# Dilated attention: the modulation's two products of a unit on column tiles, and the minima and sums in a ring of their own

## The reference

```python
DILATED_PATTERNS = ((128, 1), (512, 4), (2048, 16))
...
scores = jnp.einsum('bhrnqd,bhrnkd->bhrnqk', qb, kc, preferred_element_type=jnp.float32)
scores = jnp.where(valid, scores, NEG_INF)
m = jnp.max(scores, axis=-1, keepdims=True)
p = jnp.exp(scores - m)
denom = jnp.sum(p, axis=-1, keepdims=True)
out = jnp.einsum('bhrnqk,bhrnkd->bhrnqd', p, vc.astype(jnp.float32)) / denom
lse = (m + jnp.log(denom))[..., 0]
...
wts = jax.nn.softmax(jnp.stack(lses, axis=0), axis=0)      # over the three patterns
...
# the two layers that follow, l = 0 and 1, for c_act and cc_act
shift, scale, gate = jnp.split((c_act @ w_mod + b_mod)[:, None, :], 3, axis=-1)
```

## Time and profile before

| | |
|---|---|
| median of 3 runs | 5559.16 us (5552.03 to 5563.41) |
| time of the profiled execution | 5556.06 us |
| its span | 5554.0 us |
| TensorE busy | 4897.8 us, 88% of the span |
| mean granted TensorE clock | 0.948 |
| the stage of the change | 951 to 1428 us of the span |

### The profile page before, as it was taken

How to read it: one execution, slowest core, us unless ns; L and a number is a source line. 1 busy time by engine, 2 the same in 40 slices (tenths; PEclk the granted TensorE clock), 3 DMA queues, 4 the chain that set the end, 5 groups by cost and what they waited for, 6 DMA issues and landing times. The chain is left out here.

```text
span 5554.0 us, 67686 instructions
## 1 busy us (share of the span) xinstructions
PE 4897.8 (88%) x26653; PEld 3429.6 (62%) x26653; DVE 2387.1 (43%) x4791; ACT 1598.3 (29%) x3015; POOL 1217.2 (22%) x1271
## 2 busy tenths in 40 slices
PE   5888999999786998699999988969987899989889
PEld 2336887877675765474554576858655734544767
DVE  3221022544564465654552146334556635520554
ACT  2231101544335311222342133034112223421331
POOL 1000011000341011143884000010221438850000
PEclk8998999999897999899999999979999999999999
DMA  5001101232442000010000201230000100002122
GB/s 180 2 15 39 53 30 53 96 105 93 154 146 91 16 1 9 13 54 8 10 12 18 74 31 46 95 117 16 9 9 1 50 20 10 10 16 67 38 69 91
DMA packets 156013, 273.43 MB, mean 49 GB/s; under 512 B 12556, under 2 KB 91700, under 8 KB 155060
## 3 DMA queue, kind: packets, MB, share of 16 engines
q1 hardware_dynamic: 142164, 250.23, 13.2%
q10 hardware_dynamic: 13536, 18.88, 1.0%
HBM read 204.12 MB, written 64.95 MB: 48 GB/s over the span
## 5 line engine op out<-in xcount | busy, mean ns | idle before, releaser
L2312 POOL TENSOR_TENSOR y_t<-y_t,weight_ring 128x512 f32<-128x512 f32 x352 | 446.6, 1289 | 67.9 <-ACT weight_ring L2282 63.3
L1398 DVE TENSOR_TENSOR features_low<-h_t,features_high 128x1024 fp32r<-128x1024 f32 x260 | 304.0, 1171 | 355.1 <-ACT features_high L1363 354.4
L2330 DVE TENSOR_REDUCE y_t<-ps_max 128x2 f32<-128x1024 f32 x256 | 313.3, 1224 | 325.4 <-PE ps_max L2139 325.4
L659 PE MATMUL ps_proj<-weight_ring,h_t 128*128 128x256 f32 x2048 | 448.5, 381 | 2.7 <-PE ps_proj L659 2.2
L659 PEld LDWEIGHTS ps_proj<-weight_ring,h_t 128*128 128x128 f32 x2048 | 388.8, 191 | 57.7 <-issue 5.4
L1335 PE MATMUL ps_proj<-features_high,weights_high 128*128 128x512 f32 (+1 forms) x880 | 346.2, 393 | 59.8 <-DVE features_low L1398 30.5
L1363 ACT ACTIVATE features_high<-h_t 128x1024 fp32r<-128x1024 f32 x260 | 259.7, 1001 | 421.4 <-PE ps_proj L1335 359.5
L1335 PE MATMUL ps_proj<-features_high,weights_low 128*128 128x512 f32 (+1 forms) x880 | 340.6, 387 | 0.0
L1335 PE MATMUL ps_proj<-features_low,weights_high 128*128 128x512 f32 (+1 forms) x880 | 340.1, 387 | 0.0
L1526 PE MATMUL ps_f<-h_t,weight_ring 128*128 128x512 f32 (+1 forms) x640 | 288.7, 586 | 14.4 <-DVE state L1691 14.4
L1549 PE MATMUL ps_s<-qf,kb 64*128 64x128 f32 x3264 | 235.7, 285 | 60.9 <-DVE scores_t L1719 55.5
(11 more groups left out here) (340 smaller groups left out, 9089.6 us busy)
## 6 DMA issues: line engine op xcount, KB each, us to landing
weight_ring<-in_w_in_dram SPq DMA_DIRECT2D x40, 1024.0 KB, 5.9
weight_ring<-in_w_mod_dram SPq DMA_DIRECT2D x48, 512.0 KB, 4.0
x_rows<-h_rows SPq DMA_DIRECT2D x32, 512.0 KB, 6.1
t_rows<-t_rows SPq DMA_DIRECT2D x64, 256.0 KB, 2.3
x_res<-h_rows SPq DMA_DIRECT2D x32, 512.0 KB, 3.2
res<-result SPq DMA_DIRECT2D x48, 264.0 KB, 2.1
res_rows<-res SPq DMA_DIRECT2D x48, 264.0 KB, 3.8
h_t<-v_rows SPq DMA_DIRECT2D x3, 4096.0 KB, 13.9
```

The costliest lines, as they stand in the source:

```text
L659: mm = pe.matmul(ps[u % 4][:, 0:GC], hT[:, k, t * P:(t + 1) * P], w[:, k, :], start=(k == 0), stop=(k == KT - 1))
L1398: dve.tensor_tensor(self.fl[:, s % NB, :, 0:n], self.hT[:, k0:k0 + KS, c0:c0 + n], self.fh[:, s % NB, :, 0:n].bitcast(F32), ALU.subtract). ...
L2312: pool.tensor_tensor(acc[g % 2][:, kv, :], before, pT[s % 3][:, kv, :], ALU.add).then_inc(pa.h, 1)
L2330: ins = dve.tensor_reduce(part[:, g % 2, t, c, :].rearrange("p (v i) -> p v i", v=2)[:, :, i], pM[:, :, 0:n], AXX, ALU.max)
```

## The change

- **Column tiles.** Each of the two products of `modulate` now has a stationary operand of 64 columns (each vector repeated over 32) and writes its own half of the partitions, 0 to 63 and 64 to 127, instead of both summing into all 128. `mrow` has 128 partitions, `keep` adds all 128, and the two halves are summed later: `mr` is loaded in two transfers and `stage_output1` turns and adds it with two products instead of one transpose.
- **The ring.** Minima and sums go into `stat`, four tiles deep. `keep` of a tile's second unit copies its 16 columns into `res`, after waiting for the exponentials of that unit. The wait for the store moves from `minima` to `keep`, ahead of the copy into `res`. SP no longer waits for the exponentials.
- **Score order.** The four score products alternate between lower and upper partitions; before, two lower ones came ahead of two upper ones.
- `store_mod` has four transfers of one row each instead of two.

```diff
@@ stage_dilated
-        cvec = free[:, NM * 4 * GC:NM * 4 * GC + KT * P].rearrange("p (k v c) -> p k v c", v=2, c=P // 2)
-        mrow = env.sb(ctx, "mod2_rows", [HD + 1, 2, GC])
+        cvec = free[:, NM * 4 * GC:NM * 4 * GC + KT * HD].rearrange("p (k v c) -> p k v c", v=2, c=32)
+        mrow = env.sb(ctx, "mod2_rows", [P, 2, GC])
+        stat = env.sb(ctx, "row_stats", [P, 4, 2 * H1])
...
-                for v in range(2):
-                    sp.dma_start(mod_d[l:l + 1, 2 * c:2 * c + 2, v, :],
-                                 mrow[HD * v:HD * v + 1, y % 2, :].rearrange("p (m c) -> p m c", c=P)).then_inc(ms[y % 2].h, 16)
+                for i in range(4):
+                    sp.dma_start(mod_d[i:i + 1, 2 * y:2 * y + 2, :],
+                                 mrow[32 * i:32 * i + 1, y % 2, :].rearrange("p (m c) -> p m c", c=P)).then_inc(ms[y % 2].h, 16)
...
                 sp.wait_ge(pvc.h, pvc.at(u + 1))
-                sp.wait_ge(ex.h, ex.at(4 * (u + 1)))
...
-                for odd in range(2):
-                    for j in range(2):
+                for j in range(2):
+                    for odd in range(2):
...
-                    mm = pe.matmul(pv[u % 2][:, GC:2 * GC], cvec[:, 4 * (x % 2) + k, :, :].rearrange("p v c -> p (v c)"),
-                                   mw[:, x % NM, k, :], start=(i == 0), stop=(i == 1))
+                    mm = pe.matmul(pv[u % 2][HD * i:HD * (i + 1), GC:2 * GC], cvec[:, 4 * (x % 2) + k, :, :].rearrange("p v c -> p (v c)"),
+                                   mw[:, x % NM, k, :], start=True, stop=True)
...
@@ minima(u)
-                if hh == 0 and u >= 4:
-
-                    i = (u // 2) % 2
-                    dve.wait_ge(rs[i].h, rs[i].at(16 * (u // 4)))
...
-                                                 res[:, (u // 2) % 2, H1 * HD + h:H1 * HD + h + 1]).then_inc(sm_.h, 1)
+                                                 stat[:, (u // 2) % 4, h:h + 1]).then_inc(sm_.h, 1)
@@ keep(u)
-                row, got = mrow[:, y % 2, :], pv[u % 2][0:HD + 1, GC:2 * GC]
+                row, got = mrow[:, y % 2, :], pv[u % 2][:, GC:2 * GC]
...
+                if hh == 0 and u >= 4:
+                    i = (u // 2) % 2
+                    dve.wait_ge(rs[i].h, rs[i].at(16 * (u // 4)))
+                if hh == 1:
+                    dve.wait_ge(ex.h, ex.at(4 * (u + 1)))
+                    dve.tensor_copy(res[:, (u // 2) % 2, H1 * HD:RW], stat[:, (u // 2) % 4, :])
                 dve.tensor_copy(res[:, (u // 2) % 2, hh * 4 * HD:(hh + 1) * 4 * HD], pv[u % 2][:, 0:4 * HD]).then_inc(pvc.h, 1)
@@ stage_output1
-            sp.dma_start(mr[:, :], mod_d.rearrange("l m v p -> (l m v) p")).then_inc(md.h, 16)
+            for i in range(2):
+                sp.dma_start(mr[:, i, :], mod_d[2 * i:2 * i + 2, :, :].rearrange("v m p -> (v m) p")).then_inc(md.h, 16)
...
-                    pe.transpose(pM[:, 0:NR], mr[:, :], env.ident[0:NR, 0:NR]).then_inc(mu.h, 1)
+                    for i in range(2):
+                        mm = pe.matmul(pM[:, 0:NR], mr[:, i, :], env.ident[0:NR, 0:NR], start=(i == 0), stop=(i == 1))
+                    mm.then_inc(mu.h, 1)
```

More of the change, by code:

```diff
@@ L799, in store_mod @@
             def store_mod(y):
-                l, c = divmod(y, MH // 4)
                 sp.wait_ge(mk.h, mk.at(4 * y + 4))
-                for v in range(2):
-                    sp.dma_start(mod_d[l:l + 1, 2 * c:2 * c + 2, v, :],
-                                 mrow[HD * v:HD * v + 1, y % 2, :].rearrange("p (m c) -> p m c", c=P)).then_inc(ms[y % 2].h, 16)
+                for i in range(4):
+                    sp.dma_start(mod_d[i:i + 1, 2 * y:2 * y + 2, :],
+                                 mrow[32 * i:32 * i + 1, y % 2, :].rearrange("p (m c) -> p m c", c=P)).then_inc(ms[y % 2].h, 16)
             load_v(0)
@@ L825, in _ @@
                 sp.wait_ge(rs[i].h, rs[i].at(16 * (U // 4)))
-                sp.wait_ge(ms[i].h, ms[i].at(32 * MH // 4))
+                sp.wait_ge(ms[i].h, ms[i].at(64 * MH // 4))
         @block.tensor
@@ L935, in keep @@
                     if y >= 2:
-                        dve.wait_ge(ms[y % 2].h, ms[y % 2].at(32 * (y // 2)))
+                        dve.wait_ge(ms[y % 2].h, ms[y % 2].at(64 * (y // 2)))
                     dve.tensor_copy(row, got).then_inc(mk.h, 1)
+                if hh == 0 and u >= 4:
[4 more added lines that the diff above has]
+                    dve.tensor_copy(res[:, (u // 2) % 2, H1 * HD:RW], stat[:, (u // 2) % 4, :])
                 dve.tensor_copy(res[:, (u // 2) % 2, hh * 4 * HD:(hh + 1) * 4 * HD], pv[u % 2][:, 0:4 * HD]).then_inc(pvc.h, 1)
             dve.tensor_copy(cvec[:, :, :, :], env.csilu[:, 8:24].rearrange("p (v k) -> p k v", v=2)[:, :, :, None]
-                            .to_broadcast([P, KT, 2, P // 2])).then_inc(cw.h, 1)
+                            .to_broadcast([P, KT, 2, 32])).then_inc(cw.h, 1)
             minima(0)
@@ L960, in _ @@
                             act.activation(pr[:, u % 2, 2 * b + j, 0:w * P], sc[:, u % 2, 2 * b + j, 0:w * P], ACT.Exp,
-                                           bias=res[:, (u // 2) % 2, H1 * HD + h:H1 * HD + h + 1], scale=-1.0,
-                                           accum_out=res[:, (u // 2) % 2, H1 * HD + H1 + h:H1 * HD + H1 + h + 1])\
+                                           bias=stat[:, (u // 2) % 4, h:h + 1], scale=-1.0,
+                                           accum_out=stat[:, (u // 2) % 4, H1 + h:H1 + h + 1])\
                                .then_inc(ex.h, 1)
@@ L971, in _ @@
                                    ACT.Copy).then_inc(tc0.h, 1)
-    for s_, c_ in (*((ml[i], 16 * len(range(i, MH, NM))) for i in range(NM)), (mu, MH), (mk, U), (cw, 1), (ms[0], 8 * MH), (ms[1], 8 * MH),
+    for s_, c_ in (*((ml[i], 16 * len(range(i, MH, NM))) for i in range(NM)), (mu, MH), (mk, U), (cw, 1), (ms[0], 16 * MH), (ms[1], 16 * MH),
                    (smm, U), (sm_, 4 * U), (ex, 4 * U), (tm, 2 * U), (tc0, U), (tc1, U), (pvm, U), (pvc, U),
@@ L1013, in stage_output1 @@
         rst = env.sb(ctx, "ya_rstd", [P, 2, NT])
-        mr = env.sb(ctx, "mod2_rows", [NR, P])
+        mr = env.sb(ctx, "mod2_rows", [NR, 2, P])
         mc = env.sb(ctx, "mod_cols", [P, 2, 24, 2])
@@ L1116, in _ @@
                 if v == 2:
-                    pe.wait_ge(md.h, md.at(16))
-                    pe.transpose(pM[:, 0:NR], mr[:, :], env.ident[0:NR, 0:NR]).then_inc(mu.h, 1)
+                    pe.wait_ge(md.h, md.at(32))
+                    for i in range(2):
+                        mm = pe.matmul(pM[:, 0:NR], mr[:, i, :], env.ident[0:NR, 0:NR], start=(i == 0), stop=(i == 1))
+                    mm.then_inc(mu.h, 1)
                 if v == 4:
@@ L1212, in modulation @@
                 bt, bo = env.place["b_mod_2"]
-                link(dve.tensor_tensor(mc[:, :, :, :], pM[:, 0:96].rearrange("p (l m v) -> p l m v", l=2, v=2),
+                link(dve.tensor_tensor(mc[:, :, :, :], pM[:, 0:96].rearrange("p (v l m) -> p l m v", l=2, v=2),
                                        env.vcols[:, bt, bo:bo + 48].rearrange("p (l m) -> p l m", l=2)[:, :, :, None]
@@ L1267, in stage_output1 @@
                    (yb, NT), (yah, NT), (yal, NT), (tm, NT), (tch, NT), (tcl, NT), (sqy, NT), (iny, NT), (pwy, NT), (sqm, NT),
-                   (inm, NT), (pwm, NT), (mma, NT), (mmb, NT), (pa, 2 * NT), (pb, 2 * NT), (st, NT), (mu, 1), (md, 16), (gcs, 2),
+                   (inm, NT), (pwm, NT), (mma, NT), (mmb, NT), (pa, 2 * NT), (pb, 2 * NT), (st, NT), (mu, 1), (md, 32), (gcs, 2),
                    (gtn, 1), (gdn, 64), *((hs[i], 16 * len(range(i, NT, NX))) for i in range(NX)),
@@ L2871, in program @@
         gb_d = nc.dram_tensor("gb_rows", [S, H1 * HD], F32, kind="Internal").ap()
-        mod_d = nc.dram_tensor("mod_rows", [2, 3 * KT, 2, P], F32, kind="Internal").ap()
+        mod_d = nc.dram_tensor("mod_rows", [4, 2 * 3 * KT, P], F32, kind="Internal").ap()
         res_d = [nc.dram_tensor(f"res{p}", [S, RW], F32, kind="Internal").ap() for p in range(3)]
```

## The result

The changed kernel takes 5501.01 us, median of 4 runs (5496.05 to 5515.65), against 5556.34 (5552.03 to 5563.41): a ratio of 0.9904, 95% interval 0.9881 to 0.9926. The forecast was 5506. The profiled execution took 5496.05 us (span 5494.1), 60 us less than that of before, of which some 54 lie in the stage and 6 in the rest of the program. The rest, from the last `values` product to the end, took 4123 to 4140 us in the ten profiles of this study, the kernel before at 4130 and the changed one at 4123, so those 6 us are no effect of the change that these profiles could show. The stage is taken here from the start of its first score product to the start of its last `values` product: 472.0 us before, 418.1 after.

A forecast was written before the change was run, and what follows sets the result against it. TensorE was taken as the bound, stalled once per tile by the store wait; 27.8 + 26 - 1.5 = 52.3 us off the profiled 5556.06 gives 5503.8, or 5506 against the median of the runs; range 5492 to 5526.

The forecast's parts named there:

- What bounds the stage: TensorE, 88% busy; each tile's store wait on VectorE delays minima, exponentials, ScalarE's copy and the weight loads of `values`.
- the chain through ScalarE: Minima, exponentials and ScalarE's copy ahead of `values`: ready some 1.4 us before TensorE once the store wait is gone.
- The rival of a late load of `w_mod` behind V: Tile 20's modulation waits for its load behind V, or `keep` meets a late store; 5515 to 5524; 12 in 100.
- The moved wait: Moving the store wait from `minima` to `keep` should cover all of it, gaining 27.8 us over the stage's tiles.
- The column tiles: Modulation products run side by side, 0.27 us less per unit on TensorE, 26 us over 96 units.
- The three terms: Per unit of modulation: 0.48 us less between starts, against 0.10 for the shape change and 0.11 for the first weight load.
- The sum of the two: Gains of the moved store wait, 27.8 us, and of the modulation on column tiles, 26 us, added together.
- Score order: Alternating lower and upper score products was costed at nothing, since two already run at a time.
- The strided scores: Rival: the new order also speeds up score products of dilation 4 and 16, 41 us, giving 5465; 4 in 100.
- The small ones: Additional transfers on SP, and one more transfer and product in `stage_output1`, lose 1.5 us; the 16-column copy is covered.
- The ring: The 27.8 us gain forecast for moving the store wait from `minima` to `keep`.

The follow-up runs named there:

- e3: The changed kernel with the two lower-half score products ahead of the two upper-half ones, as before; 5506.68 us in one run.
- e5: The changed kernel with the keys of every score product read without a stride (other data, timing only); 5479.6 us in one run.
- e6: The changed kernel with keys and queries of the score products both read without a stride (other data, timing only); 5458.16 us in one run.
- e4: The changed kernel with both modulation products of a unit on the same column tile, so not side by side; 5536.27 us in one run.
- e1: The changed kernel without the ring, in the old score order, so column tiles alone; 5561.74 us against 5559.95 for the kernel before, ratio 1.0005.
- e9: Label not defined in the text; apparently the kernel before with only the ring of minima and sums added; 5529.41 us, ratio 0.9942.

## Why the prediction was right

- **What bounds the stage**: right. TensorE, with one stall per tile that comes from the store through the minima and ScalarE. With the wait moved no other took its place. The slack of the chain through ScalarE was put at 1.4 us and is 1.37. The rival of a late load of `w_mod` behind V did not come, that stretch is busy for all of its 29.46 us, but here luck had a part: the load landed 0.11 us before TensorE reached it in this profile, 0.70 before in e3, and in e5 and e6, whose units are shorter, TensorE did stall for it. The prediction named this rival and gave it 12 in 100 together with another; it did not work out how near it was.
- **The moved wait, 27.8 us**: the stretches shrank by 53.2 us, and 0.29 for each of the 92 units in them is 26.7, which leaves 26.5. The ring alone gave 30 us by the runs and 28.4 in its stage. By stretch the forecast was 13.9, 11.2, 6.5 and 18.2 for the last four, and 14.2, 11.3, 7.1 and 18.8 came. Only at tiles 0 and 1 it was too high, 3.0 against 1.8: the lower clock of the start held on longer (until 27 us behind the stage's first product instead of 23; 0.71 for the stretch, 0.82 before).
- **The column tiles, 0.27 us per unit**: 0.29. The three terms came as put: 0.48 less between the starts, 0.10 for the change of shape, 0.11 for the uncovered weight load; the score order adds 0.01. The Trainium skill says that a change of the tiling mode drains TensorE ("TensorEngine Tiling (Array Packing)", Tiling Modes) and gives no duration; the trace agrees that it costs something, these 0.10 and 0.11 us. e4 shows what they cost when nothing pays for them: 0.14 us per unit.
- **The sum of the two** was right for the change as a whole, and says nothing of its parts. The text said that TensorE is the bound "once the store's wait is gone", but did not draw the consequence that e1 shows: in a tile that waits for the store the column tiles gain nothing.
- **Score order, nothing**: right (e3). The strided scores did not speed up.
- **The small ones, 1.5 us lost**: too high. The last four transfers take 1.19 us on SP where the last two took 1.14, not twice as long, and the next stage's first load is issued 4.2 us behind the start of the last `values` product instead of 4.1. The new copy of 16 columns takes 0.17 us as put and is covered. What the additional transfer and product in `stage_output1` cost can't be told from the spread of the rest of the program.
- **The size of the whole**: the stage is 53.9 us shorter where 52.3 were forecast. The ring was put 1.3 us too high, the column tiles 1.9 too low (0.29 for 96 units is 27.8), and the loss by the small ones 1.5 too high, so the errors partly cancel; that 5506 lies within 5 us of 5501.01 is closer than the interval of the measurement (41 to 66 us saved) can confirm.

## What to carry to other kernels

Look for the loop that a wait closes, and list what stands in it: shortening an engine's work outside the loop buys nothing until the loop is broken, however busy that engine is (e1, dilation 1 and 16). Give small results that are written early a buffer of their own when they share one with results that are stored late; the wait then moves to the late writer. Look also at the loads that were just in time: with shorter units the next wait is theirs (e5, e6). Products with few stationary columns belong side by side on column tiles, and as many in one group as there are, since each group pays for its change of shape; here this was seen with 32-bit products of 256 columns.

## What was not expected of the hardware

- A change between full width and column tiles costs 0.2 us at the full clock, half of it the next weights' load. Eight rows on four column tiles take 0.64 us, as long as four rows on two (0.65).
- The mean granted clock was 0.75 over 122 us in e1, with TensorE busy for 92% of them by its rows, where the kernel before had 0.98 at 94%; once down, it stayed at the lower level for 41 us of unbroken work. The changed kernel and e9, in which TensorE's rows leave no gap there, had 1.00. Why e1 fell and stayed down is left open.
- A stride of 4 in the moving operand makes the products of 256 columns of 32-bit data 1.7 times as long (2.19 against 1.31 us for eight rows), and weights with a stride of 16 cost the 128-column ones 0.43 us of 1.14.
